# Second attention of a two-layer step: the next pair's decode scores, sigmoids and weights ahead of the next prompt block's, on TensorE, ScalarE and VectorE

## The chip, the cores and the metric

The kernel runs on one core of one Trainium2 chip. The metric is the device time of one execution in microseconds; three runs of the kernel before gave 1647.73, 1647.85 and 1648.43 us.

## The reference, cut to what matters

A two-layer transformer step for 512 prompt tokens and for 8 decode sequences of 16 new tokens each, over a cache of 1024 positions. Layer one has differential attention, layer two the stick-breaking attention that this change touches:

```python
def stick_breaking_attention(q, k, v, q_pos0):
    ...
    for start in range(0, Tq, Q_BLOCK):
        stop = min(start + Q_BLOCK, Tq)
        k_end = max(1, min(Tk, q_pos0 + stop - 1))
        qb, kb, vb = q[:, start:stop], k[:, :k_end], v[:, :k_end]
        z = jnp.einsum('bqhd,bkhd->bhqk', qb, kb).astype(jnp.float32) * scale
        q_pos = q_pos0 + jnp.arange(start, stop)
        mask = jnp.arange(k_end)[None, :] < q_pos[:, None]
        log_1m = jnp.where(mask, jax.nn.log_sigmoid(-z), 0.0)
        suffix = lax.cumsum(log_1m, axis=3, reverse=True) - log_1m
        a = jnp.where(mask, jnp.exp(jax.nn.log_sigmoid(z) + suffix), 0.0)
        outs.append(jnp.einsum('bhqk,bkhd->bqhd', a.astype(v.dtype), vb))
```

So a weight is sigmoid(z) times the product of sigmoid(-z) over all later keys. Prompt and decode tokens go through it apart, with 16 heads of 64. Around it lie projections and two feed-forward blocks, in float32.

## The kernel before

Each engine has its program written out by hand, and semaphores tie them together. The part concerned is the second attention (class `Attention`, object `tb`), at 998 to 1158 us of the profiled execution. It has two kinds of work, woven into each other.

**Decode.** 16 pairs (`N_PAIRS`): pair n is sequence n // 2 and half of the heads, n % 2. Its 1024 cached keys and values come as four loads of 1 MiB (two of keys, two of values) into a ring of ten places (SP issues them, `loads`). The steps of a pair:
- `pe_s(n)`: scores on PE, z(n). 16 matmuls per pair over the cached keys (L1260, two halves), then a last group over the 16 new keys (L1269, L1273). The groups wait for several things: the copies of the last pair's transposed weights (`wev`, `wne`), since the transposes used the same banks, and, the last group alone, for DVE's copies `wn` (L1668, tile swn) and `o` (L1682, L1683, tile qks) of the pair in work and the one before it, since those lie in the bank that the last group writes.
- `act_sx(n)`: two sigmoids on ACT over 1040 keys: u of -z into sw (L1460), x of z into sp or sp_b (L1462).
- `dve_sprod(n)`: on DVE the running product backwards over sw (L1659, a scan; **S(n)** in what follows), and its product with x (L1661, semaphore p).
- `pe_w1`, `pe_w2`, `pe_wn`: transposes of the weights (L1283, L1300, L1294); ACT copies them out (`act_w1`, `act_w2`, L1471, L1477, tiles swt and work), DVE the new keys' part (`dve_wn`, L1668).
- `pe_v(n)`: 64 small matmuls of weights and values (L1319) and 4 for the new keys (L1327); `act_osb` copies the result, `pe_o` transposes it (L1339), `dve_o` copies it into qks (L1682, L1683).

**Prompt.** 32 blocks (`STEPS`): block k is 128 queries against (k % 4 + 1) * 128 keys, for two heads. The steps: `pe_ps` (scores, L1204, L1210), `act_pu` and `act_px` (two sigmoids, L1410, L1419), `dve_prod` (two scans L1621 and a product L1627), `pe_pt` (transposes in rounds of up to four, L1225), `act_pt` or, for one round in six, `dve_pt` (copies into wt, L1439 and L1447), `pe_pv` (L1238), and every fourth block `act_po` (L1453).

The order is set by three loops over n: `pe_b`, `act_b` and `dve_b`. A turn of the loops, here a slot, holds blocks k + 1 and k + 2 (k = 2n) and the values of pair n and the scores of pair n + 1. In an even slot blocks k + 1 and k + 2 have 256 and 384 keys, in an odd slot 512 and 128; two slots make a cycle. DVE's copies `wn` and `o` of a slot are issued between the scans and the product of block k + 1:

```python
def dve_new(self, n):
    self.dve_wn(n)
    if n > 0:
        self.dve_o(n - 1)
...
self.dve_prod(ch, k + 1, lambda: self.dve_new(n))
```

sw exists once, so u(n + 1) waits for the product of pair n (semaphore p); sp has two buffers.

Of the kernel before, what the change touches and what calls it, by code (L numbers as in the profile page):

```python
# [35 lines left out]
N_PAIRS = DEC_B * G  # L36
# [30 lines left out]
def program(nc, a_x, a_w, a_ka, a_va, a_ks, a_vs, a_masks, a_const, a_small, o_y, o_ka, o_va, o_ks, o_vs):  # L67
    with ExitStack() as ctx:
# [150 lines left out]
        def split_hi(act, ph, j, s, free=None):  # L219

            u = j + units[ph][0]
            if isinstance(u, int) and u >= UNITS:
                return
            raw_ready(act, ph, j, s)
            if free is not None:
                act.wait_ge(*free)
            elif not (isinstance(u, int) and u < 2):

                act.wait_ge(mm, tiles_before(ph, j - 1))
            nc.scalar.activation(w_hi[s][:, :, :], w_raw[:, s, :, :], ACT.Copy).then_inc(hi_done, 1)  # L230
# [9 lines left out]
        def split_lo(dve, ph, j, s):  # L240

            u = j + units[ph][0]
            if isinstance(u, int) and u >= UNITS:
                return
            dve.wait_ge(hi_done, split_count(ph, j))
            nc.vector.tensor_tensor(w_lo[s][:, :, :], w_raw[:, s, :, :], w_hi[s][:, :, :].bitcast(F32),  # L246
                                    ALU.subtract).then_inc(lo_done, 1)
# [836 lines left out]
        STEPS = KT * QB  # L1084
# [5 lines left out]
        class Attention:  # L1090
# [285 lines left out]
            def pe_b(self, pe):  # L1376
                for n in range(N_PAIRS):
                    k = 2 * n
                    rounds = self.slot_rounds(n)
                    self.pe_ps(k + 1)  # L1380
                    if n % 2 == 1:
                        self.pe_pv(k - 2)
                    for j, r in rounds[:2]:
                        self.pe_pt(j, r)
                    self.pe_w1(n)
                    self.pe_w2(n)
                    self.pe_wn(n)
                    if n > 0:
                        self.pe_o(n - 1)
                    for j, r in rounds[2:]:  # L1390
                        self.pe_pt(j, r)
                    if n + 1 < N_PAIRS:
                        self.pe_ps(k + 2)
                        self.pe_s(n + 1)
                        self.pe_v(n)
                    if n > 0:
                        self.pe_pv(k - 1)
                    if n % 2 == 1:
                        self.pe_pv(k)
                self.pe_v(N_PAIRS - 1)  # L1400
                for r in range(2):
                    self.pe_pt(STEPS - 1, r)
                self.pe_o(N_PAIRS - 1)
                self.pe_pv(STEPS - 1)
# [145 lines left out]
            def act_b(self, act, first, stored):  # L1550
                self.act_pu(0)
                self.act_px(0)
                self.act_sx(0)
                for n in range(N_PAIRS):
                    k = 2 * n
                    rounds = self.slot_rounds(n)
                    if n == N_PAIRS - 5:
                        for w in stored:
                            act.wait_ge(*w)
                    self.act_pu(k + 1)  # L1560
                    self.act_px(k + 1)
                    if n % 2 == 0:
                        self.act_pt(*rounds[0])
                    self.act_w1(n)
                    self.act_w2(n)
                    for j, r in rounds[1:2]:
                        self.act_pt(j, r)
                    for j, r in rounds[2:]:
                        self.act_pt(j, r)
                    if k + 2 < STEPS:  # L1570
                        self.act_pu(k + 2)
                        self.act_px(k + 2)
                    if n >= N_PAIRS - 5:
                        self.act_hi(n - (N_PAIRS - 5))
                    if n + 1 < N_PAIRS:
                        self.act_sx(n + 1)
                    else:
                        act.wait_ge(*self.last_used("w_hi0"))
                        split_hi(act, first, 0, 0)
                    if n + 1 < N_PAIRS:  # L1580
                        self.act_osb(n)
                    if n % 2 == 0 and n > 0:
                        self.act_po(n // 2 - 1)
                self.act_osb(N_PAIRS - 1)
                for r in range(2):
                    self.act_pt(STEPS - 1, r)
                self.act_po(KT - 1)
                self.act_hi(5)
                act.wait_ge(self.s["o"], N_PAIRS)
                for g in range(G):  # L1590
                    self.act_his(g)
                for t in range(6, KT):
                    self.act_hi(t)
# [184 lines left out]
            def dve_b(self, dve, ch, first, stored):  # L1778
                dve.wait_ge(kq["qev"], KT)
                nc.vector.memset(pw1[:, :, SEQ:SEQ + 4], 1.0)  # L1780
                self.dve_q(0, slice(KT // 2, KT))
                for n in range(N_PAIRS):
                    k = 2 * n
                    if n % 2 == 1:
                        self.dve_pt(k - 1)
                    self.dve_prod(ch, k + 1, lambda: self.dve_new(n))
                    if n % 2 == 0 and n + 2 < N_PAIRS:
                        self.dve_q(n // 2 + 1)
                    if k + 2 < STEPS:
                        self.dve_prod(ch, k + 2)  # L1790
                    if n + 1 < N_PAIRS:
                        self.dve_sprod(ch, n + 1)
                dve.wait_ge(*self.last_used("w_lo0"))
                split_lo(dve, first, 0, 0)
                dve.wait_ge(self.s["pvs"], N_PAIRS)
                self.dve_lo(0)
                self.dve_lo(1)
                dve.wait_ge(self.s["pv"], STEPS)
                for w in stored:
                    dve.wait_ge(*w)  # L1800
                self.dve_lo(2)
                self.dve_o(N_PAIRS - 1)
                for t in range(3, 6):
                    self.dve_lo(t)
                for g in range(G):
                    self.dve_los(g)
                for t in range(6, KT):
                    self.dve_lo(t)
# [477 lines left out]
```

## Time and profile before

| | us |
|---|---|
| median of three runs | 1647.85 |
| lowest, highest | 1647.73, 1648.43 |
| the profiled execution, its time | 1649.32 |
| its span | 1647.5 |
| PE busy in the span | 1616.3 (98%) |
| DVE busy in the span | 1151.9 (70%) |
| ACT busy in the span | 740.6 (45%) |
| second attention, between the scans S(1) and S(15) | 1004.6 to 1146.1 |

The clock that was granted to PE is 1.00 of full speed over the whole span. Times of rows are microseconds from the start of the span. PE is the matmul engine, PEld its weight loads (which overlap the matmuls), DVE is VectorE, ACT is ScalarE, POOL is GpSimd, SP issues loads. A row of a timeline merges equal instructions that follow each other (x8), and its duration reaches from the first start to the last end. A prompt block's L1210, L1204 and so on are lines of the kernel before. "issue" as a releaser means that the engine waited for nothing that the profile shows. Of a wait for several semaphores, the one that came last is named.

### The profile page before, as it was taken

The page shows a single profiled execution, that of the slowest core. Times are in us where ns is not written, and L with a number is a line of the kernel's source. Part 1 is how long each engine was busy: PE and PEld are TensorE (multiplying, and loading weights), DVE is VectorE, ACT ScalarE, POOL GpSimd, SP SyncE. Part 2 cuts the span into 40 slices and gives each one's busy share as a digit, 9 for nine tenths or more (in the row PEclk, how much of TensorE's full clock was granted, in tenths as well). Part 3 has the DMA queues.
Part 4 walks back from the last instruction along what each step waited for, and adds up shares of the span by engine and source line. Part 5 has one row for each costly group of instructions (what it writes and reads, how often), then busy time and mean ns, then how long its engine had stood idle before and what let it go on. Part 6 is the DMA issues. An engine that isn't in the chain of part 4 may idle for free.

```text
span 1647.5 us, 31458 instructions
## 1 busy us (share of the span) xinstructions
PE 1616.3 (98%) x13140; PEld 1483.3 (90%) x13140; DVE 1151.9 (70%) x1605; ACT 740.6 (45%) x1228; POOL 145.7 (9%) x123
## 2 busy tenths in 40 slices
PE   8999999999999999999999999999999999999999
PEld 6888766699999999999999896666999999999999
DVE  5765477668984797488742328989689848974874
ACT  5444366765541344134432215768555413531441
POOL 0000000012210011012000000000122201110110
PEclk9999999999999999999999999999999999999999
DMA  7133899941222122222244358996412221221222
GB/s 286 52 111 132 350 418 418 419 160 52 86 94 103 52 78 103 77 78 78 103 166 140 112 209 360 420 418 288 167 66 89 95 85 52 103 102 53 78 103 90
DMA packets 39596, 265.45 MB, mean 161 GB/s; under 512 B 4256, under 2 KB 4640, under 8 KB 10272
## 3 DMA queue, kind: packets, MB, share of 16 engines
q1 hardware_dynamic: 36720, 252.95, 39.8%
q0 software_dynamic: 2736, 10.49, 1.8%
q8 instruction: 105, 1.72, 0.4%
q14 instruction: 35, 0.29, 0.0%
HBM read 247.69 MB, written 15.73 MB: 160 GB/s over the span
## 4 chain that ended last, share of the span: by engine, by line
PE 85%; DVE 8%; DMA 3%; issue 2%; ACT 2%; SPq 0%; DVEq 0%; ACTq 0%
PE ps L584 30%; PE ps L799 28%; PE ps L268 5%; PE ps L269 4%; PE ps L270 4%; PE ps L1260 2%; PE ps L1319 2%; DVE s_lo L748 2%; PE ps L611 2%; PE ps L1204 2%; DMA kv<-in_v_a 1%; PE ps L1238 1%; DMA xT<-in_v_a 1%; PE ps L1225 1%; DVE pw L1621 1%
## 5 line engine op out<-in xcount | busy, mean ns | idle before, releaser
L230 ACT ACTIVATE w_hi<-w_raw 128x2048 fp32r<-128x2048 f32 x55 | 105.1, 1910 | 190.3 <-PE ps L584 158.5
L246 DVE TENSOR_TENSOR w_lo<-w_raw,w_hi 128x2048 fp32r<-128x2048 f32 x55 | 126.0, 2291 | 71.4 <-ACT w_hi L230 71.4
L744 ACT ACTIVATE s_hi<-t 128x512 fp32r<-128x512 f32 x176 | 109.4, 626 | 144.6 <-PE ps L799 65.8
L799 PE MATMUL ps<-hs_hi,s_hi 128*128 128x320 f32 x528 | 163.8, 310 | 0.0
L799 PE MATMUL ps<-hs_hi,s_lo 128*128 128x320 f32 x528 | 163.2, 309 | 0.0
L799 PE MATMUL ps<-hs_lo,s_hi 128*128 128x320 f32 x528 | 163.1, 309 | 0.0
L584 PE MATMUL ps<-gu_hi,w_hi 128*128 128x320 f32 x692 | 157.9, 309 | 0.2
L584 PE MATMUL ps<-gu_lo,w_hi 128*128 128x320 f32 x692 | 157.7, 309 | 0.0
L584 PE MATMUL ps<-gu_hi,w_lo 128*128 128x320 f32 x692 | 157.6, 309 | 0.0
L748 DVE TENSOR_TENSOR s_lo<-t,s_hi 128x512 fp32r<-128x512 f32 x176 | 132.8, 760 | 5.4 <-ACT s_hi L744 4.6
L268 PE MATMUL ps<-w_hi,h_hi 128*128 128x512 f32 x320 | 126.8, 396 | 8.1 <-DVE h_lo L300 8.1
L657 DVE TENSOR_TENSOR sg<-ps,rows 128x640 f32<-128x640 f32 x47 | 38.7, 823 | 128.6 <-PE ps L584 128.6
L269 PE MATMUL ps<-w_lo,h_hi 128*128 128x512 f32 x320 | 125.8, 393 | 0.0
L270 PE MATMUL ps<-w_hi,h_lo 128*128 128x512 f32 x320 | 125.6, 393 | 0.0
L744 ACT ACTIVATE s_hi<-w_raw 128x512 fp32r<-128x512 f32 x132 | 82.6, 626 | 86.3 <-PE ps L584 48.6
L584 PEld LDWEIGHTS ps<-gu_hi,w_hi 128*128 128x128 f32 x692 | 115.6, 188 | 0.7 <-DVE gu_lo L976 0.7
L584 PEld LDWEIGHTS ps<-gu_lo,w_hi 128*128 128x128 f32 x692 | 115.7, 188 | 0.0
L584 PEld LDWEIGHTS ps<-gu_hi,w_lo 128*128 128x128 f32 x692 | 115.7, 188 | 0.0
L799 PE MATMUL ps<-ho_hi,s_hi 128*128 128x320 f32 x352 | 109.5, 311 | 1.2 <-DVE up L948 0.8
L799 PE MATMUL ps<-ho_hi,s_lo 128*128 128x320 f32 x352 | 108.8, 309 | 0.0
L799 PE MATMUL ps<-ho_lo,s_hi 128*128 128x320 f32 x352 | 108.7, 309 | 0.0
L913 POOL TENSOR_TENSOR up<-up,p 128x320 f32<-128x320 f32 x44 | 57.4, 1305 | 512.9 <-DVE up L948 512.9
(298 smaller groups left out, 3995.9 us busy)
## 6 DMA issues: line engine op xcount, KB each, us to landing
w_raw<-in_w SPq DMA_DIRECT2D x99, 1024.0 KB, 4.8
kv<-in_k_a SPq DMA_DIRECT2D x12, 1024.0 KB, 16.1
kv<-in_v_a SPq DMA_DIRECT2D x12, 1024.0 KB, 16.7
kv<-in_v_s SPq DMA_DIRECT2D x12, 1024.0 KB, 12.6
kv<-in_k_s SPq DMA_DIRECT2D x12, 1024.0 KB, 15.0
xT<-in_k_a SPq DMA_DIRECT2D x8, 1024.0 KB, 17.4
xT<-in_k_s SPq DMA_DIRECT2D x8, 1024.0 KB, 11.7
work<-in_v_a SPq DMA_DIRECT2D x7, 1024.0 KB, 14.9
```

The costliest lines, as they stand in the source:

```text
L230: nc.scalar.activation(w_hi[s][:, :, :], w_raw[:, s, :, :], ACT.Copy).then_inc(hi_done, 1)
L246: nc.vector.tensor_tensor(w_lo[s][:, :, :], w_raw[:, s, :, :], w_hi[s][:, :, :].bitcast(F32), ALU.subtract).then_inc(lo_done, 1)
L268: nc.tensor.matmul(out, s_hi, m_hi, start=first, stop=False, skip_group_check=True)
L269: nc.tensor.matmul(out, s_hi, m_lo, start=False, stop=False, skip_group_check=True)
L270: return nc.tensor.matmul(out, s_lo, m_hi, start=False, stop=last, skip_group_check=True)
L584: last = nc.tensor.matmul(ps[:, banks_n[n] + h, 0:HALF], w[:, k, n * P:(n + 1) * P], m[:, slot(m, k), h * HALF:(h + 1) * HALF], start=(k = ...
L611: last = nc.tensor.matmul(ps[:, OUT[n] + h, 0:HALF], w[:, k, n * P:(n + 1) * P], m[:, slot(m, k), h * HALF:(h + 1) * HALF], start=(k == 0 ...
L657: ch.link(nc.vector.tensor_tensor(halves(sg[:, n, :]), y, halves(rstd_row), ALU.mult))
L744: nc.scalar.activation(s_hi[i][:, :, :], factor(j % 2, i), ACT.Copy).then_inc(hi_done, 1)
L748: nc.vector.tensor_tensor(s_lo[i][:, :, :], factor(j % 2, i), s_hi[i][:, :, :].bitcast(F32), ALU.subtract)\
L799: last = nc.tensor.matmul(ps[:, bank[i], 0:HALF], w[:, p, :], m[:, p, :], start=(i < 3 and p == 0 and a == 0), stop=(p == 3 and a == 2), s ...
L913: nc.gpsimd.tensor_tensor(up[:, s, HALF:TOK], up[:, s, HALF:TOK], p5[:, s, :], ALU.add)\
```

## The change

In all three loops the pair's work for n + 1 goes ahead of the prompt block k + 2: on PE the scores of pair n + 1 ahead of the scores of block k + 2, on ACT the pair's two sigmoids ahead of the block's two, on DVE S(n + 1) and its product ahead of the block's scans and product. In PE's loop the number of transposing rounds ahead of the weights' transposes is now 2 in even slots and 1 in odd ones (it was 2 in all), so in odd slots both rounds of block k, whose product DVE now makes later, come behind them. Nothing is added or left out.

```diff
@@ -1377,21 +1377,22 @@
                 for n in range(N_PAIRS):
                     k = 2 * n
                     rounds = self.slot_rounds(n)
+                    ahead = 1 + (n + 1) % 2
                     self.pe_ps(k + 1)
                     if n % 2 == 1:
                         self.pe_pv(k - 2)
-                    for j, r in rounds[:2]:
+                    for j, r in rounds[:ahead]:
                         self.pe_pt(j, r)
                     self.pe_w1(n)
                     self.pe_w2(n)
                     self.pe_wn(n)
                     if n > 0:
                         self.pe_o(n - 1)
-                    for j, r in rounds[2:]:
+                    for j, r in rounds[ahead:]:
                         self.pe_pt(j, r)
                     if n + 1 < N_PAIRS:
+                        self.pe_s(n + 1)
                         self.pe_ps(k + 2)
-                        self.pe_s(n + 1)
                         self.pe_v(n)
                     if n > 0:
                         self.pe_pv(k - 1)
@@ -1567,14 +1568,13 @@
                         self.act_pt(j, r)
                     for j, r in rounds[2:]:
                         self.act_pt(j, r)
-                    if k + 2 < STEPS:
+                    if n + 1 < N_PAIRS:
+                        self.act_sx(n + 1)
                         self.act_pu(k + 2)
                         self.act_px(k + 2)
                     if n >= N_PAIRS - 5:
                         self.act_hi(n - (N_PAIRS - 5))
-                    if n + 1 < N_PAIRS:
-                        self.act_sx(n + 1)
-                    else:
+                    if n + 1 == N_PAIRS:
                         act.wait_ge(*self.last_used("w_hi0"))
                         split_hi(act, first, 0, 0)
                     if n + 1 < N_PAIRS:
@@ -1786,10 +1786,10 @@
                     self.dve_prod(ch, k + 1, lambda: self.dve_new(n))
                     if n % 2 == 0 and n + 2 < N_PAIRS:
                         self.dve_q(n // 2 + 1)
+                    if n + 1 < N_PAIRS:
+                        self.dve_sprod(ch, n + 1)
                     if k + 2 < STEPS:
                         self.dve_prod(ch, k + 2)
-                    if n + 1 < N_PAIRS:
-                        self.dve_sprod(ch, n + 1)
                 dve.wait_ge(*self.last_used("w_lo0"))
                 split_lo(dve, first, 0, 0)
                 dve.wait_ge(self.s["pvs"], N_PAIRS)
```

DVE, at the border of an even and an odd slot (sw and sp are the pair's tiles, pw and pp the prompt block's; the scans of L1621 and L1659 are printed here as SCALAR_TENSOR_TENSOR; the line of the wt copy is one higher after the change):

```order
 L1627 TENSOR_TENSOR pp<-pp,pw 128x2x256
 L1640 TENSOR_SCALAR qs<-qks 64x8x16 x2
+L1659 SCALAR_TENSOR_TENSOR sw<-sw 128x1040
+L1661 TENSOR_TENSOR sp<-sp,sw 128x1040
 L1621 SCALAR_TENSOR_TENSOR pw<-pw 128x384 x2
 L1627 TENSOR_TENSOR pp<-pp,pw 128x2x384
-L1659 SCALAR_TENSOR_TENSOR sw<-sw 128x1040
-L1661 TENSOR_TENSOR sp<-sp,sw 128x1040
-L1447 COPY wt<-ps 128x512
+L1448 COPY wt<-ps 128x512
 L1621 SCALAR_TENSOR_TENSOR pw<-pw 128x512 x2
 L1668 TENSOR_SCALAR swn<-ps,const 128x128
```

The pair's scan and product stood behind the block of 384 keys and stand ahead of it now. The wt copy, the scans of the 512 block and the swn copy follow in both, now directly behind the 384 block.

PE, an odd slot (pp is the prompt block's weights, sp the pair's, osb the last pair's output; L1260 begins the next pair's scores):

```order
 L1210 MATMUL ps<-steps 128x64 x4
 L1238 MATMUL ps<-wt,v 64x128 x2
-L1225 MATMUL ps<-const,pp 128x128 x8
+L1225 MATMUL ps<-const,pp 128x128 x4
 L1283 MATMUL ps<-const,sp 128x128 x4
 L1300 MATMUL ps<-const,sp 128x128 x4
 L1294 MATMUL ps<-const,sp 128x128
 L1339 MATMUL ps<-const,osb 128x128
-L1225 MATMUL ps<-const,pp 128x128 x2
-L1204 MATMUL ps<-qkp 128x128 x2
-L1210 MATMUL ps<-steps 128x64 x4
+L1225 MATMUL ps<-const,pp 128x128 x6
```

Of the three rounds of transposes only the first stays ahead of the pair's; the six of block k go behind the transpose of osb. The scores of the 128 block (L1204, L1210) leave this place, and come back behind the pair's scores.

ACT, the end of the same slot, before and after (sw and sp_b are the pair's sigmoids, pw and pp the prompt block's; all lines are one higher after the change):

```order
L1439 ACTIVATE wt<-ps 128x512
L1439 ACTIVATE wt<-ps 128x256
L1410 ACTIVATE pw<-ps 128x2x128
L1419 ACTIVATE pp<-ps 128x2x128
L1460 ACTIVATE sw<-ps 128x1040
L1462 ACTIVATE sp_b<-ps 128x1040
```

```order
L1440 ACTIVATE wt<-ps 128x512
L1440 ACTIVATE wt<-ps 128x256
L1461 ACTIVATE sw<-ps 128x1040
L1463 ACTIVATE sp_b<-ps 128x1040
L1411 ACTIVATE pw<-ps 128x2x128
L1420 ACTIVATE pp<-ps 128x2x128
```

The pair's two sigmoids pass those of the 128 block; the copies into wt stay where they were.

## Rows read from the trace of the kernel before

**Rows 1.** The page: the span, and busy time of an engine, its share.

```profile
span 1647.5 us, 31458 instructions
...
PE 1616.3 (98%) x13140; PEld 1483.3 (90%) x13140; DVE 1151.9 (70%) x1605; ACT 740.6 (45%) x1228; POOL 145.7 (9%) x123
```

**Rows 2.** Windows: busy us (x instructions) of each engine, granted clock, DMA share, GB/s.

```profile
1000.00:1010.00 10.00, 8.91 (x148) 5.95 (x148) 9.85 (x13) 7.34 (x11) 0.00 (x0) 1.00 1.00 419
...
1110.00:1120.00 10.00, 10.00 (x172) 7.60 (x168) 9.82 (x13) 7.59 (x13) 0.00 (x0) 1.00 1.01 418
...
1130.00:1140.00 10.00, 9.77 (x167) 7.35 (x166) 9.82 (x14) 7.15 (x14) 0.00 (x0) 1.00 0.95 392
1140.00:1150.00 10.00, 10.00 (x163) 6.98 (x164) 8.99 (x12) 8.74 (x15) 0.00 (x0) 1.00 0.11 43
```

**Rows 3.** Instructions of line L1659, the long scan S: duration in ns, first and last start.

```profile
L1659 DVE TENSOR_TENSOR_SCAN sw<-sw x15: 2316/2317/2319, 1004.6 to 1146.1; 128x1040 f32<-128x1040 f32 x15
```

**Rows 4.** Waits, 998 to 1158 us: who waited for whom, us in total, times, longest.

```profile
PEld ps L1269 <- DVE swn L1668: 5.3, 7, 0.8
...
DVE swn L1668 <- PE ps L1339: 2.2, 7, 0.3
...
PE ps L1210 <- issue: 1.4, 1, 1.4
...
PE ps L1283 <- DVE sp_b L1661: 1.3, 4, 0.4
...
PE ps L1225 <- issue: 1.1, 1, 1.1
```

**Rows 5.** Timeline of DVE: start us, duration us, instruction; in brackets idle time before it.

```profile
1107.39 2.32 DVE L1659 TENSOR_TENSOR_SCAN sw<-sw 128x1040 f32<-128x1040 f32 x1
...
1123.95 1.81 DVE L1621 TENSOR_TENSOR_SCAN pw<-pw 128x384 f32<-128x384 f32 x2
...
1126.66 2.32 DVE L1659 TENSOR_TENSOR_SCAN sw<-sw 128x1040 f32<-128x1040 f32 x1
...
1130.29 0.69 DVE L1447 COPY wt<-ps 128x512 f32<-128x512 f32 x1
...
1133.75 0.23 DVE L1683 TENSOR_SCALAR qks<-ps 64x64 f32<-64x64 f32 x1
...
1136.26 2.32 DVE L1659 TENSOR_TENSOR_SCAN sw<-sw 128x1040 f32<-128x1040 f32 x1
1138.61 1.24 DVE L1661 TENSOR_TENSOR sp_b<-sp_b,sw 128x1040 f32<-128x1040 f32 x1
1139.77 1.27 DVE L1621 TENSOR_TENSOR_SCAN pw<-pw 128x256 f32<-128x256 f32 x2
```

**Rows 6.** Timeline of PE, four places of the second attention.

```profile
999.72 0.92 PE L1204 MATMUL ps<-qkp 64*128 64x384 f32 x4
...
1021.37 1.92 PE L1260 MATMUL ps<-kv,qs 128*32 128x512 f32 x16
...
1131.82 0.49 PE L1204 MATMUL ps<-qkp 64*128 64x128 f32 x4
...
1132.30 1.92 PE L1260 MATMUL ps<-kv,qs 128*32 128x512 f32 x16
1134.12 0.25 PE L1269 MATMUL ps<-qks,qs 128*32 128x16 f32 x5
...
1138.58 1.09 PE L1225 MATMUL ps<-const,pp 128*128 128x128 f32 x8
```

**Rows 7.** Timeline of ACT, three places of the second attention.

```profile
1002.78 1.05 ACT L1460 ACTIVATE sw<-ps 128x1040 f32<-128x1040 f32 x1 [0.53 <-PE ps L1273]
...
1023.52 1.04 ACT L1460 ACTIVATE sw<-ps 128x1040 f32<-128x1040 f32 x1 [0.39 <-PE ps L1273]
...
1139.77 0.60 ACT L1419 ACTIVATE pp<-ps 128x512 f32<-128x512 f32 x1 [0.48 <-PE ps L1225]
...
1140.74 0.60 ACT L1471 ACTIVATE swt<-ps 128x512 f32<-128x512 f32 x1
```

## The prediction

> **What bounds the kernel now.** I read the page first: the span is 1647.5 us and PE is busy for 98% of it [rows 1]. The share says little about this change, which touches one stage only, the second attention. So next came the windows of 10 us through that stage [rows 2]. From 1000 to nearly 1140 us the transfers run at a share of 1.0 of the 16 DMA engines, PE is busy for 8.9 to 10 us of each 10 in the windows shown, and DVE for 9.0 to 9.9. Three resources are nearly full, so the order of the work decides what waits. The instructions of one line show the pace: the long scan of each pair, S(n), stands 15 times between 1004.6 and 1146.1 us [rows 3]. That is 141.5 us for 14 pairs, or 7 cycles of two pairs (prompt blocks repeat their sizes every 4, so every two pairs).
>
> The timeline of DVE gives the pace without disturbance: S(11) starts at 1107.39 and S(15) at 1146.1 [rows 3, 5], so 38.7 us for two cycles, 19.35 each. Seven of these are 135.5, and 141.5 were used. The other 6.0 us come with five gaps in the middle of PE's matmul groups, 1.1 to 1.4 us each, for which the profile has no releaser ("issue") [rows 4]. Inside the undisturbed 19.35 us DVE idles only 0.3 us, before the copy swn, for PE's transpose of the last output [rows 4]; DVE with its 19.0 us of work is the bound, and PE is right behind it.
>
> **What the change does to a cycle.** No instruction is added or taken away, and the queues of SP and POOL are the same, so no load is issued in another order. I call a slot even or odd by n. On DVE the products of a prompt block change places with the long scan and product of the next pair. In the even slot the block that moves back has 384 keys and costs 2.71 us (its scan at 1123.95, S(13) at 1126.66 [rows 5]); in the odd slot it has 128 keys.
>
> Gain: the pair's weights are ready before that block, so PE no longer waits for them (4 times, 1.3 us in all, at L1283 [rows 4]), and the 0.3 us of DVE behind that wait can go. That is worth 0.3 times 7, or 2 us, if nothing else is late.
>
> Loss: the odd slot. There PE's scores s(n+1) end with a group (L1269, L1273) that writes where the last output is read, and waits for DVE's swn and qks copies. In the kernel before, this wait is there already in seven slots and ends last each time: 5.3 us in total [rows 4]. Those copies stand on DVE behind the wt copy and the scans of the 512 block. The 384 block now lies ahead of all these, and behind S. So from S(odd) to the end of the qks copies DVE must do, without a hole: S and its product 3.51 (1136.26 to 1139.77), the 384 block 2.71, and from the wt copy to the end of qks 3.69 (1130.29 to 1133.75 plus 0.23) [rows 5]. PE's last group starts 0.14 after that (1133.98 to 1134.12 [rows 5, 6]). Part A is 3.51 + 2.71 + 3.69 + 0.14 = **10.05 us**.
>
> From there the path runs over PE and ACT to the next S(odd), through the even slot. The row before shows nearly the same string: from the group at 1134.12 over the values and the prompt products to the next block's scores and eight transposes (1138.58, 1.09 long), then ACT's second sigmoid at 1139.77 and its copy swt at 1140.74, which ends at 1141.34 [rows 6, 7]. That is 7.22 us. The scores of the 128 block now lie in it too: 0.48 (1131.82 to 1132.30 [rows 6]). PE then starts s(n+1) after a hand-over of 0.1 (as from PE's last transpose, 1139.67, to ACT at 1139.77). From the start of s to the sigmoid u on ACT it is 2.15 (1021.37 to 1023.52 [rows 6, 7]), u takes 1.04, and another 0.1 passes until S starts. Part B is 7.22 + 0.48 + 0.10 + 2.15 + 1.04 + 0.10 = **11.09 us**.
>
> In the kernel before, this loop is closed too, but without the 2.71 it hides behind DVE's own work. Now A + B = 21.14 us, more than DVE's 19.0: the cycle is set by a chain over all three engines, and DVE idles some 2.1 us in each. Against 19.35 that is +1.79, and seven cycles make **+12.5 us**.
>
> Start: S(1) no longer stands behind the 384 block. It may start once u(1) has ended; u(1) started at 1002.78 before [rows 7] and ended at 1003.8, and s(1) now starts up to 0.9 earlier, since the scores of the 384 block (from 999.72 [rows 6]) no longer precede it. So S(1) starts between 1002.9 and 1003.8 in place of 1004.6: -0.8 to -1.7. I take **-1**.
>
> End: after S(15) the 384 block, the wt copy and the last 512 block are still to come on DVE, so the last transposes and the output projection come up to 2.71 later, counted from S(15). PE has its own work meanwhile, some of which hides it: 0 to +2.7. I take **+2**, since PE ends this stage on that block.
>
> The gaps: before, five of them cost 6.0 us, all of their length, because PE was full. Now PE idles in part A for a while before the blocked group, and is on the path in part B, about half of the cycle. Between 0 and 6.0 I take the middle, **3**, so -3 against before. What makes the gaps no row tells; they lie where the transfers run at 1.0. The Trainium skill, "Runtime: NRT & Kernel Launch", section "Instruction fetch mechanics", states that an engine fetches its program in blocks of 256 instructions over a DMA queue of its own, and that this is mostly hidden. If the gaps were such fetches and hidden in the new order, the sum would be 3 us lower; no row here names their cause.
>
> The cover of everything else: ACT is busy for about 7 of 10 us [rows 2], so two sigmoids that change places cost nothing there as long as the block behind them isn't the next thing DVE takes; it is taken 3.5 us (S and its product) later, against 1.9 us of ACT's work. Transfers: 8 loads of 1 MiB a cycle at 419 GB/s need 20.0 us, less than 21.1; they stay hidden. The rest of the kernel only shifts.
>
> **Sum:** 12.5 - 1 + 2 - 3 = **+10.5 us**. The profiled execution took 1649.32 us, so it would be 1659.8; the median of the three runs is 1647.85, 1.5 us below it, and from that the forecast is **1658.3 us**. Bounds: the gaps 0 or 6.0 (3 either way), start and end together 2 either way, and 0.2 us a cycle for hand-overs (two of the 0.1 above). Those seldom add up; the forecast's own range is 1653 to 1664.
>
> **Rivals.**
> 1. *Faster.* The loop doesn't close as I walked it: the blocked group holds up less behind it, and DVE stays unbroken. Then the cycle is DVE's 19.0, seven of them give -2.3, start and end +1, the gaps -3: -4.3, so 1643.5 us. It decides as soon as A + B is under 19.35, so if the 2.71 of the 384 block were not in A. For it: the two waits on the pair's weights do exist. Against it: the seven waits of L1269 on DVE are in the trace, and nothing can pass them. 0.11.
> 2. *No change.* Transfers set the pace: 20.0 us a cycle by their rate, and the mean before is 141.5/7 = 20.2. Then the order has no effect beyond the ends, and the time is 1648 to 1650. For it: the share of 1.0. Against it: two cycles ran at 19.35 while the share was 1.0, and by 1140 the share is 0.11 [rows 2] with S(15) still to come, so data lay ready early. 0.08.
> 3. *Slower still.* The gaps cost their full 6.0, and the prompt sigmoids, now behind the pair's on ACT, make DVE wait as well, by 0.3 to 0.5 us a cycle: 10.5 + 3 + 3 = 16.5, so 1664 us or more. For it: ACT waits for PE's scores in nearly every slot. Against it: the 3.5 us of cover above. 0.11.
>
> **Chances.** The forecast has 0.70. A measurement of this kernel can tell 0.2%, or 3.3 us, from no change; the forecast and rival 3 are slower by more, rival 1 faster by more, rival 2 within. So slower 0.81, same 0.08, faster 0.11. The range takes the forecast's own, a little towards rival 2, and the near edge of rival 3: 1651 to 1664.
>
> **What would show it.** In the new profile the long scan should stand 15 times from about 1003.6 to about 1155 us (seven cycles of 21.14 and 3 us of gaps: 151), with two steps a cycle, one of about 11.5 and one of about 9.6 us. DVE should wait for ACT's u at L1659 in nearly every slot, some 2 us a cycle in all, 12 to 15 us in total. PEld L1269 should wait for DVE's copies for over 1 us in each odd slot. The waits on the pair's weights (L1283) and the 0.3 us at swn should be gone, and PE's busy share lower. I am wrong if the steps stay at 9.6 and 9.7, or if L1659 never waits; if the cycle is right and the total isn't, the gaps or the end were mis-sized.

## The result, and the profile after

The change made the kernel slower, and by more than forecast.

| | before | changed |
|---|---|---|
| median, us | 1648.0 (4 runs) | 1667.98 (4 runs) |
| lowest, highest | 1647.73, 1648.43 | 1661.91, 1671.11 |
| the profiled execution, its time | 1649.32 | 1661.91 |
| its span | 1647.5 | 1660.1 |

The ratio is 1.0118, with a 95% interval of 1.0103 to 1.0133. The forecast was 1658.3 us with a range of 1651 to 1664: the sign is right, the time 9.7 us short, and the median outside the range. The profiled execution is the fastest of the four, so its rows explain 12.6 us (1661.91 - 1649.32), and the rest has to be found in other executions. They differ by 9 us, where the four of the kernel before differ by less than 1; in the later series of 15 to 22 executions that kernel has a spread of its own, 1644.0 to 1649.9 us. Three single executions of the kernel before and two of its variants took two to five times as long (3208, 4082 and 7936 us) and are left out of every number below.

The page after answers to [rows 1]; PE has 6.3 us more of busy time and the same share.

```profile
span 1660.1 us, 31458 instructions
...
PE 1622.6 (98%) x13140; PEld 1486.8 (90%) x13140; DVE 1151.4 (69%) x1605; ACT 739.8 (45%) x1228; POOL 145.5 (9%) x123
```

The long scan, by its line, answers to [rows 3] (here S(0) at 991.2 is counted too; S(1) stands at 1003.36):

```profile
L1659 DVE TENSOR_TENSOR_SCAN sw<-sw x16: 2323/2325/2326, 991.2 to 1156.4; 128x1040 f32<-128x1040 f32 x16
its engine sat idle before it (us, times) until:
  ACT sw L1461: 20.7, 16
```

S(15) starts at 1156.41 in place of 1146.05, and DVE now waits for ACT's sigmoid ahead of every single one. The timeline of DVE over a cycle, from S(4) to S(6), answers to [rows 5], and under it stands the one row of PE's timeline that follows the copies (start us, duration us, in brackets idle time before it):

```profile
1036.08 2.33 DVE L1659 TENSOR_TENSOR_SCAN sw<-sw 128x1040 f32<-128x1040 f32 x1 [0.37 <-ACT sw L1461]
...
1045.65 2.32 DVE L1659 TENSOR_TENSOR_SCAN sw<-sw 128x1040 f32<-128x1040 f32 x1 [1.83 <-ACT sw L1461]
1048.01 1.24 DVE L1661 TENSOR_TENSOR sp<-sp,sw 128x1040 f32<-128x1040 f32 x1
1049.17 1.80 DVE L1621 TENSOR_TENSOR_SCAN pw<-pw 128x384 f32<-128x384 f32 x2
...
1055.45 0.23 DVE L1683 TENSOR_SCALAR qks<-ps 64x64 f32<-64x64 f32 x1
1055.71 1.23 DVE L1627 TENSOR_TENSOR pp<-pp,pw 128x1024 f32<-128x1024 f32 x1
1057.31 2.33 DVE L1659 TENSOR_TENSOR_SCAN sw<-sw 128x1040 f32<-128x1040 f32 x1 [0.38 <-ACT sw L1461]
```

```profile
1055.83 0.25 PE L1269 MATMUL ps<-qks,qs 128*32 128x16 f32 x5 [0.27 <-DVE qks L1683]
```

From S(5) to the end of the copies DVE works without a hole: 1045.65 to 1055.68, then 0.15 us to PE's group at 1055.83. That is part A, 10.18 us. In stretches without disturbance the steps alternate, 11.66 from an odd S to an even one and 9.53 back, so a cycle is 21.19 and part B the other 11.01. Before, the cycle was 19.35 by the prediction's rows (19.28 in its least disturbed steps, 9.60 and 9.68).

The waits, 995 to 1175 us, answer to [rows 4] (who waited for whom, us in total, times, longest):

```profile
DVE sw L1659 <- ACT sw L1461: 18.5, 15, 2.2
...
PEld ps L1269 <- DVE swn L1668: 10.8, 7, 1.7
...
PE ps L1269 <- DVE qks L1683: 4.6, 7, 0.8
...
PE ps L1238 <- issue: 3.3, 2, 2.4
...
PE ps L1210 <- issue: 1.3, 1, 1.3
...
DVE swn L1668 <- PE ps L1339: 0.9, 3, 0.3
```

The wait of L1269 for DVE's copies has doubled, from 5.3 to 10.8 us over the same seven slots. No row with L1283 is left. Two windows answer to [rows 2] (busy us of PE, PEld, DVE, ACT, POOL, then granted clock, DMA share, GB/s): DVE is down from 9.85 to 7.91 us in the first of them, and the loads, which had a share of 0.11 left from 1140 us on, have 0.49 there.

```profile
1000.00:1010.00 10.00, 8.59 (x141) 5.76 (x142) 7.91 (x11) 6.94 (x10) 0.00 (x0) 1.00 1.01 425
...
1140.00:1150.00 10.00, 8.82 (x154) 6.14 (x154) 9.44 (x11) 6.36 (x12) 0.00 (x0) 1.00 0.49 205
```

So the profiled 12.6 us are: S(1) earlier by 1.2; seven cycles at 21.19 in place of 19.35, +12.9; what is left of the stretch from S(1) to S(15) over its seven cycles, 153.05 - 148.3 = 4.7 in place of 6.0, -1.3; the end from S(15) to the next phase's first matmul, 14.2 in place of 12.1, +2.1.

### The profile page after: what moved, and what is told of

It is laid out like the page before. It is cut to its first block, busy times and chain, and to the rows that moved or that the text cites. A ratio compares the mean times of both kernels' runs of the same rounds, so it can differ in the third digit from the quotient of the medians.

```text
span 1660.1 us, 31458 instructions
## 1 busy us (share of the span) xinstructions
PE 1622.6 (98%) x13140; PEld 1486.8 (90%) x13140; DVE 1151.4 (69%) x1605; ACT 739.8 (45%) x1228; POOL 145.5 (9%) x123
## 4 chain that ended last, share of the span: by engine, by line
PE 86%; DVE 8%; issue 3%; ACT 2%; DMA 0%; DVEq 0%; SPq 0%; ACTq 0%
PE ps L584 30%; PE ps L799 28%; PE ps L268 4%; PE ps L269 4%; PE ps L270 4%; PE ps L1319 2%; PE ps L1260 2%; PE ps L1204 2%; DVE s_lo L748 2%; PE ps L1238 2%; PE ps L611 2%; PE ps L1225 1%; DVE pw L1621 1%; ACT pp_a L1425 1%; PE ps L1283 1%
```

## The experiments

Twelve more runs follow, the changed kernel again and eleven variants. Times are medians; "before" is the kernel before, run on the same chip in the same job, 1647.8 to 1647.9 in all of them (the three jobs were on three chips).

### The changed kernel again

> The changed kernel once more, for how its executions spread. Its profiled execution took 1661.9 us, the three others 1666.7 to 1671.1, while the kernel before has all of its runs within 0.7 us. Theory A (the longer loop over DVE, PE and ACT alone): it is the same work in the same order each time, so the runs gather near 1662, and the others were chance. Theory B (the loop leaves PE idle more, and something on PE makes the holes longer in some executions: gaps without a releaser, or a lower granted clock after them): they spread again over 8 us or more, and the profile shows gaps of over 2 us or a granted clock under 1.00 somewhere in the second attention, and the excess there is the excess of that execution.

Measured: 1666.15 us (1662.89 to 1670.25, 5 runs), ratio 1.011 [1.0092, 1.0127]. The profiled execution took 1669.81, 7.9 us more than the first one, with the same program. Here are its waits and two windows:

```profile
DVE sw L1659 <- ACT sw L1461: 18.1, 15, 2.2
...
PE ps L1327 <- issue: 3.2, 1, 3.2
PE ps L1238 <- issue: 3.0, 1, 3.0
...
PE ps L1210 <- issue: 2.3, 1, 2.3
```

```profile
1010.00:1020.00 10.00, 6.02 (x124) 3.93 (x124) 8.45 (x11) 3.45 (x7) 0.00 (x0) 0.95 1.01 418
...
1130.00:1140.00 10.00, 7.05 (x46) 5.95 (x50) 4.20 (x10) 2.62 (x6) 0.00 (x0) 0.66 0.73 297
```

The undisturbed steps are 11.66 and 9.54, as in the first profile, so the chain is the same; yet S(1) to S(15) took 161.5 us, 13.2 over seven cycles. All of it lies in three of the short steps, each with one gap of PE in it:

| step | us, in place of 9.54 | lost | gap of PE | clock after it |
|---|---|---|---|---|
| S(2) to S(3) | 14.52 | 5.0 | 3.19 at 1015.5 | half for 3.4 us |
| S(8) to S(9) | 12.04 | 2.5 | 2.33 at 1086.2 | full |
| S(12) to S(13) | 15.24 | 5.7 | 2.96 at 1129.8 | half for 6.8 us |

In these steps a gap costs its whole length, and the granted clock sometimes falls to its lower level (1.2 GHz), in the gap or right behind it. The first profile has gaps of 1.26 and 2.42 us at the same two instructions as the last two rows, and those steps lost 1.4 and 2.8. It also has two that lost nothing, 0.84 us at L1238 behind S(5) and 0.64 at L1319 behind S(9): both lie in part A, and the steps around them are 11.66 us as without a gap. The first of them in PE's timeline:

```profile
1049.05 0.66 PE L1238 MATMUL ps<-wt,v 128*64 128x128 f32 x7 [0.84 <-issue]
```

### Only the even slots, and only the odd ones

```diff
                     if n + 1 < N_PAIRS:
-                        self.pe_s(n + 1)
-                        self.pe_ps(k + 2)
+                        if n % 2 == 0:
+                            self.pe_s(n + 1)
+                            self.pe_ps(k + 2)
+                        else:
+                            self.pe_ps(k + 2)
+                            self.pe_s(n + 1)
```

The same condition stands around the pair's work in the loops of ACT and DVE. In the second kernel it is `n % 2 == 1`, and two rounds of transposes stay ahead everywhere; the first kernel keeps the changed order's rounds, one ahead in odd slots.

> Only the even slots have the new order (S ahead of the 384 block on PE, ACT and DVE), the odd ones have the old one. Theory A says the loss hangs on the 384 block between S(odd) and the copies swn and qks that the last group of the scores waits for: the two steps of a cycle from scan S to scan S are about 12.2 and 8.4 us, together 20.5 to 21 in place of 19.35, and the time is 8 to 13 us over the kernel before. The rival (the order on ACT, sigmoids of the pair ahead of the prompt's in every slot) expects half of the loss in each half, so some 5 to 7 us.

> Only the odd slots have the new order (S ahead of the 128 block), the even ones have the old one, and two rounds of transposes go ahead of the weights in all slots. Theory A: nothing new stands between S(odd) and the copies that L1269 waits for, so cycles stay at 19.3 to 19.6 us and the time is within 3 us of the kernel before (1648 to 1651). The rival (order on ACT) expects 5 to 7 us more than before, as in the other half.

Measured: even slots alone 1658.35 us (1658.07 to 1658.52, 4 runs), ratio 1.0065 [1.0049, 1.008]; odd slots alone 1651.58 (1650.74 to 1652.99, 10 runs), ratio 1.0025 [1.0015, 1.0034]. The row of DVE's waits on the sigmoid, for the even kernel and then for the odd one (the lines are higher by the added conditions):

```profile
DVE sw L1666 <- ACT sw L1465: 14.5, 8, 2.1
```

```profile
DVE sw L1666 <- ACT sw L1465: 4.8, 8, 2.2
```

The 384 block, which the even slots move behind S, carries the loss: +10.5 of the 18, with undisturbed steps of 12.31 and 8.42, a cycle of 20.73. The odd slots' 128 block adds less: +3.8, above the 3 that was expected, with steps of 10.78 and 8.94, a cycle of 19.72 where at most 19.6 was expected. By undisturbed cycles the halves add up: 1.45 and 0.44 us over 19.28, and 1.91 together. The rival, half of the loss in each half, falls.

### The copies ahead of the 512 block

```diff
                     if n % 2 == 1:
                         self.dve_pt(k - 1)
-                    self.dve_prod(ch, k + 1, lambda: self.dve_new(n))
+                        self.dve_new(n)
+                    self.dve_prod(ch, k + 1, None if n % 2 == 1 else lambda: self.dve_new(n))
```

> The changed kernel, but in odd slots DVE makes the copies swn and qks directly behind the wt copy, ahead of the two scans of the 512 block (2.36 us). Theory A: part A of the loop is 2.36 us shorter, the loop is 18.8 us and DVE's own 19 us of work and small waits bound it again: cycles of 19.4 to 20.2 in place of 21.2, so 7 to 12 us under the changed kernel. If the wait for those copies is not what sets the cycle, the cycles stay at 21.2.

Measured: 1654.94 us (1654.1 to 1655.48, 4 runs), ratio 1.0043 [1.0027, 1.0058], 11.2 us below the changed kernel in the same job. With the two scans of the 512 block (2.4 us) behind the copies, part A is shorter and the cycle falls to 20.2 us (S at 1079.06, 1099.30, 1119.50). It doesn't fall by the full 2.4, because another wait takes the place: PE's transposes of the 384 block wait for its product, and the scores stand behind them. From S(9) at 1088.10 the product ends at 1094.41, the six transposes start at 1094.46 and the last group at 1097.29. So part A is 9.19 in place of 10.18, and with the 11.01 of part B that makes 20.20.

```profile
DVE sw L1659 <- ACT sw L1461: 13.4, 8, 2.1
...
PEld ps L1225 <- DVE pp L1627: 6.7, 12, 1.0
```

So the wait of the last group of s on DVE's copies, with the 384 and 512 blocks in front of them, is what binds the changed kernel.

### Both orders with light loads

```diff
                     src = self.ka[2 * n + h, :, :] if kind == "k" else self.va[n, :, h * 2048:(h + 1) * 2048]
+                    if self.b and self.before[o]:
+                        dst, src = dst[:, 0:512], src[:, 0:512]
```

These two leave out three quarters of 54 of the 64 loads of the second attention, so they compute its decode part from partly stale keys and values; the instructions of PE, ACT and DVE are those of the full kernels.

> The changed kernel, but in the second attention only the first 10 of the 64 loads of cached keys and values bring all their bytes; the other 54 bring the first quarter (keys and values beyond it are stale, so the decode part of the output is another one). The order of all instructions is unchanged. Theory B says that PE's gaps without a releaser are waits for the next 256 instructions of its program, late because the transfers fill the queues: with the transfers far below their rate the gaps go, the granted clock stays at 1.00 and the runs stop spreading (all within 2 us), with cycles of 21.2 us and S(1) to S(15) 148 to 149 us. If the gaps belong to the order itself, or to the engine, they stay, 2 to 3 us each, and the runs spread over 5 us or more.

> The same cut of the loads in the kernel before. Theory B: the five gaps of 1.1 to 1.4 us go, cycles of 19.3 us, S(1) to S(15) 135.5 us in place of 141.5, and the time 5 to 6.5 us under the kernel before (about 1642). Against light_after the difference is the loop alone, 12.9 us for the seven cycles and 1 for both ends: 13 to 15 us. If the gaps stay, the time is within 1 us of the kernel before.

Measured: changed order 1658.76 us (1657.88 to 1659.62, 5 runs), ratio 1.007 [1.0057, 1.0083]; order before 1642.85 (1642.28 to 1645.61, 11 runs), ratio 0.9975 [0.9967, 0.9984]. The scan's row of the changed order, then of the order before:

```profile
L1661 DVE TENSOR_TENSOR_SCAN sw<-sw x16: 2324/2325/2326, 991.0 to 1152.3; 128x1040 f32<-128x1040 f32 x16
```

```profile
L1661 DVE TENSOR_TENSOR_SCAN sw<-sw x16: 2316/2318/2325, 991.0 to 1139.3; 128x1040 f32<-128x1040 f32 x16
```

The gaps are nearly gone. In the order before two are left, of 0.4 and 0.3 us; in the changed order this one:

```profile
PE ps L1329 <- issue: 0.7, 1, 0.7
```

The stretch S(1) to S(15) is 149.2 us in the changed order and 135.45 in the order before, the latter exactly the 135.5 that the prediction worked out. This pair weighs the chain alone: 15.9 us, of which the profiles account for 14.9 (13.7 in the stretch, -0.8 at the start and +2.0 at the end); 13 to 15 were expected. It also weighs the gaps: 1647.9 - 1642.9 = 5.0 us before, 1666.15 - 1658.76 = 7.4 changed (the latter across two jobs). The spread of the changed kernel, 7 to 9 us, shrinks to 1.7, and that of the order before from 4.9 to 3.3: most of what the executions differ by is their gaps.

### The instructions shifted

A few matmuls of 16 columns, put ahead of the first attention. They shift every later instruction of PE by 64, 128 or 192 places. With 96 of them they do something more: they take 2.56 us from 170.02, and right behind them the granted clock was at its lower level for 3.4 us. S(1) then stands 3.1 us later in the order before (1007.65 for 1004.57); with 32 and 64 it is 0.7 and 0.4.

```diff
+            for _ in range(64):
+                nc.tensor.matmul(ps[:, 7, 0:16], steps[:, 0:P], steps[:, 0:16], start=True, stop=True)
             ta.pe_ps(0)
```

> The changed kernel with 64 tiny matmuls (16 columns, a result that nobody reads) on PE ahead of the first attention, 128 instructions with their weight loads: half of a block of 256. The first attention hides their 2 to 4 us behind its transfers. Theory B: the gaps stand where a block of the program ends, so they move to other places in the second attention, half a block earlier in its work; their number and length, the spread and the median change by some us in either direction (1655 to 1670), while undisturbed cycles stay at 21.2. If the gaps belong to places of the work, they stay at the same lines of the same pairs (L1327 of pair 1, L1210 of the 256 block of slot 8, L1238 of slot 11).

> The kernel before with the same 64 matmuls. Theory B: the five gaps move to other lines, and the time changes by up to 4 us in either direction; undisturbed cycles stay at 19.3. Otherwise the gaps stay at L1327 of pair 1, L1238 and L1210, and the time is within 1 us of the kernel before.

> The changed kernel with 32 small matmuls (64 instructions of PE, some 2 us at most, in a place where the first attention waits for transfers) ahead of the first attention. Question: is the extra cost of the gaps in the changed order (7.4 us over its light version, against 5 us in the order before) a property of the order, or of where the gaps fall among PE's instructions? With a shift of 64 matmuls the two orders gave 1664.5 and 1648.5: over their light versions 5.7 and 5.6. Theory (place): the gaps stand at other instructions, cost 2 to 9 us over 1658.8 whatever the order, so 1661 to 1668, and the excess over light is as often smaller as larger than that of the order before at the same shift. Rival (order): the longer wait of PE in the changed order makes the gaps longer at each shift: 1664 to 1670, and the excess over light is larger than that of the order before at this shift and at 96.

> The order before with the same 32 matmuls. Theory (place): 1645 to 1650, gaps at other instructions, 2 to 7 us over the 1642.9 of the light version. Rival (order): 1647 to 1648.5 as without a shift, each gap below 1.5 us.

> The changed kernel with 96 small matmuls (192 instructions). Theory (place): 1661 to 1668, excess over light about that of the order before at this shift. Rival (order): 1664 to 1670, excess over light larger than in the order before again.

> The order before with the same 96 matmuls. Theory (place): 1645 to 1650. Rival (order): 1647 to 1648.5. In both the difference between the two orders stays 13 to 19 us at every shift, since 13.7 us of it are the chain over the three engines, which no gap makes.

Measured (medians; the stretch is S(1) to S(15) in the one profiled execution, less that of the light kernel of the same order, 135.45 or 149.18; the last column is each kernel's largest gap of PE in that stretch):

| matmuls added | before, us | changed, us | difference | stretch over light: before, changed | largest gap: before, changed |
|---|---|---|---|---|---|
| none | 1647.9 | 1666.2 | 18.3 | 6.0; 3.9 and 12.3 | 1.4; 2.4 and 3.2 |
| 32 | 1649.09 | 1661.37 | 12.3 | 7.0; 6.8 | 2.2; 3.3 |
| 64 | 1648.49 | 1664.49 | 16.0 | 4.7; 5.0 | 2.1; 2.5 |
| 96 | 1652.86 | 1667.42 | 14.6 | 5.8; 6.8 | 1.8; 2.9 |

Ratios to before, in the order of the rows: order before 1.001 [1.0001, 1.0019], 1.0006 [0.9998, 1.0015], 1.0038 [1.0024, 1.0051]; changed order 1.0085 [1.0072, 1.0098], 1.0105 [1.0091, 1.012], 1.0119 [1.0103, 1.0135].

The gaps move to other instructions with each shift. In the order before, shifted by 32 matmuls, they stand at L1225 and L1238 (waits of PE, as above):

```profile
PE ps L1225 <- issue: 2.4, 2, 2.2
...
PE ps L1238 <- issue: 2.0, 1, 2.0
```

The rival, that the changed order makes gaps cost more at every shift, falls: at 32 and 96 matmuls the changed kernel has 2.6 and 8.7 us over its light version, the order before 6.2 and 10.0, and gaps of over 2 us occur in the order before too. The longest gap is longer in the changed order at each placement; yet the sums come out alike as far as four placements can tell. Their mean is 6.1 us in the changed order and 6.7 before by the medians, 6.7 and 5.9 by the stretches of the profiled executions (no light kernel was run with a shift, and at 96 matmuls some 3 us of the medians are the later start, in both orders). The difference of the two orders is 15.3 us in the mean, close to the 15.9 of the light pair, with 12.3 and 18.3 as its ends. Two expectations missed: the difference at 32 fell below the 13 given, and 1652.86 lies above the 1650 given, mostly by those 3 us.

## Why the prediction missed, step by step

**The bound and the loop: right.** Part A was 10.05 and is 10.18, part B 11.09 and is 11.01, the cycle 21.14 and is 21.19. Seven cycles were to cost 12.5 us; they cost 12.9 by the profile and 13.7 in the light pair. Half a microsecond of this is the cycle before, which is 19.28 in the light kernel and not 19.35 (the fourth of the steps that the prediction took it from is 9.79 in place of 9.68). S(1) is 1.2 us earlier (1 forecast), the end 2.1 later (2 forecast). The steps are 11.66 and 9.53 (11.5 and 9.6), the waits on L1283 are gone, PEld L1269 waits up to 1.7 us. DVE's waits at L1659 are 18.5 us in all, above the 12 to 15: 2.2 a cycle, and the first one and the gaps on top. "Mid" shows by intervention that the blocked group is the link, "even" and "odd" that the 384 block is most of its price.

**The failed step: the gaps.** The prediction had: "Between 0 and 6.0 I take the middle, 3", so -3 against before; the runs gave +2.4 in its place at this kernel's placement (7.4 us against 5.0 in the light pairs), and about 0 in the mean of four placements (6.1 against 6.7). The reason given was that PE's idle time in part A would hide some of the gaps, and that is so. Before the change the gaps that cost time were the four behind S(2), S(5), S(8) and S(9), 1.5 us or so each; the one of 1.09 us behind S(1) cost nothing (that step is 9.50 us, and 9.48 in the light kernel). Two of the four now fall in part A, and all of the 3.1 us that their steps had lost is back. In the five full profiles of the changed order (two unshifted, three shifted) four gaps of over 0.35 us stand in part A, 2.3 us together, and each step from an odd S to an even one is 11.53 to 11.67 us, gap or not.

What failed is that the term let the other gaps keep their length and number. In part B, on the path, the same five profiles have twelve, 26.2 us together. At the instructions of the kernel before, the one behind S(8) went from 1.40 to 1.26 and 2.33 us, the one behind S(2) from 1.24 to none and 3.19, and a new one of 2.42 and 2.96 stands behind S(12); the clock's lower level came on top in two steps. What was hidden in A was paid again in B. Why they are longer there stays open. With a change of 0 the forecast would have been 1661.3 us, and still 4.9 under the 1666.15: half of that is the chain, half this placement.

**The bounds were too narrow.** The upper end took the 6.0 us of one execution as the most that gaps can cost. That was what they cost at the old places. At the places of the changed kernel they cost 7.4 in the median, 12.3 in the stretch of one profiled execution, and at a shift of 32 matmuls 2.6. The remainder of the miss: 1666.15 - 1647.8 = 18.3 is 15.9 by the chain (forecast 13.5) and 2.4 by the places of the gaps (forecast -3).

**The rivals.** "Faster" needed A + B under 19.35 and is refuted by the steps. "No change" too: with the loads cut to a quarter (a share of 0.34 from 1020 to 1140 us) the two orders are still 15.9 us apart, so transfers don't set the pace. "Slower still" gave the right side and size, 1664 or more, for half the right reason: the gaps cost in full, but the prompt's sigmoids held DVE up only twice, for 0.8 and 2.2 us, and not by 0.3 to 0.5 in each cycle. Both times it was right behind a gap of PE (those that ended at 1083.63 and 1127.28), so no part of the loss is ACT's order.

**What makes the gaps** was left open with a rule beside it. The light pair shows that they need full transfers: the same instructions at a DMA share of 0.3 to 0.4 have 0.7 us of them in all. The shifts show that their place goes with the count of PE's instructions, and the traces show it to the instruction. Number all records of PE in order of time (weight loads, matmuls, and those of its sequencer): the 14 profiles of this case have 58 gaps of over 0.35 us without a releaser, 43 of them in the second attention, and every one lies ahead of a record whose number is 193, 194 or 195 above a multiple of 256. And around the gaps the trace has packets of a queue of its own kind; this is the view of the DMA queues of the changed kernel, run again, from 1016 to 1017.2 us (packets, MB, share of 16 engines):

```profile
q8 instruction: 1, 0.02, 5.3%
```

One packet, 5.3% of 16 times 1.2 us, so 1.02 us long; the gap that began at 1015.49 ended at 1018.67. The one in the window from 1130 to 1131.5 goes with the gap that ended at 1132.76. Each of the 43 gaps in the second attention ended 1.3 to 1.7 us after the end of such a packet. In the order before the packet had begun 1.0 to 1.4 us ahead of the gap; here, at 1016.15, it began 0.7 us after it, so a longer gap is a packet that came later. In the order before, 20 such packets stand between 998 and 1158 us, and five of them had a gap.

```profile
q8 instruction: 20, 0.33, 0.8%
```

PE has 5036 weight loads and matmuls in that stretch (2520 and 2516 by the window), about 250 for each packet. The Trainium skill, "Runtime: NRT & Kernel Launch", section "Instruction fetch mechanics", states that an engine fetches blocks of 256 instructions over its own DMA queue and that this is mostly hidden. The trace agrees with the first half by the step of 256; the second holds for 15 of these 20 packets, and over the light kernels the rest cost 2.6 to 10 us, by order and placement. So the gaps are waits for blocks of the program that come late when the loads fill the DMA engines. In the light kernel of the order before the packets took as long (20 of them, 0.9% of the 154 us from 998 to 1152, so 1.1 us each), so it is not the packet's own time that grew under full transfers; how long a request waits ahead of it no row shows.

**Open.** Why one execution has a gap of 2.42 us and another of 2.96 at the same instruction, and why the longest gaps are longer in the changed order, isn't settled. That a sequencer blocked at L1269 asks for its next block later would fit the second, but no run tested it. None of the versions here beats the kernel before; the nearest, with only the odd slots changed, is 3.8 us behind.

## What to carry to other kernels

Before work is pulled ahead of other work on a full engine, list what lies behind the work that is pushed back, and walk the loop over all engines back to its own start: 2.7 us that had been hidden closed a loop of 21.2 us where DVE's 19.0 had set the pace. The walk from rows was right to 0.1 us a cycle; the disturbances were not. A term that no row explains should be weighed by where it would fall in the new order. Here idle time did hide what fell in it, but what fell on the path grew by as much. And its bound should be taken wider than one kernel at one placement shows: 64 instructions more in front moved the changed kernel by 5 us.

## What the runs showed of the hardware

- With the transfers at a share of 1.0, PE stops in the middle of matmul groups for 0.4 to 3.3 us, two to five times per stretch S(1) to S(15), always at the same count within 256 of its instructions, and goes on 1.3 to 1.7 us after a packet of its instruction queue. At light loads stops of at most 0.7 us are left, and the kernel before is 5 us faster.
- In the 14 profiles the two attentions have 23 gaps of 1.8 us and more. With 13 of them (1.81 to 3.29 us) the granted clock fell to its lower level, for 3.4 or 6.8 us, in the gap or up to 1.4 us after it; with the other 10 (1.80 to 2.65) it stayed, and so it did after all gaps of 0.9 to 1.64 us. It also fell right behind the 96 added matmuls of 16 columns, with no gap ahead of them. In the changed kernel's first profile the lower level shows at 215 us, in the first attention, and seems to have cost nothing, as S(0) stands at 991.2 us there and at 991.7 before:

```profile
215.00:220.00 5.00, 4.73 (x18) 2.94 (x18) 1.22 (x1) 0.75 (x2) 0.00 (x0) 0.50 1.02 423
```

- A few tens of matmuls that do nothing changed the time of a 1650 us kernel by -4.8 to +5.0 us, more than the 3.8 us of the odd slots' new order. A comparison at one placement mixes the two.
